# A two-layer SSM and attention kernel: one gate job of the first layer moved into the opening

## The chip, the cores and the metric

The kernel runs on one core of one Trainium2 chip. The metric is the device time of one execution in microseconds (us): the median of several runs. Everything is float32.

## The reference

A token block of 512 x 2048 goes through two layers of a first block (an S5 state-space mixer beside a differential attention, joined by an output projection) and through a second block (gated delta rule beside sliding-window attention). Only the start of layer one matters here, cut to:

```python
c_act = silu(c)
mod = c_act @ w_ada[l] + b_ada[l]                 # w_ada: 2048 x 6144
shift, scale, gate = split(mod, 3)
h = rms_norm(x, norm_g[l]) * (1 + scale) + shift
proj = h @ w_in[l]                                # 2048 x 6144
u, z_s, q, k, v, z_a = split(proj, ...)           # 1024 columns each
y_s = s5_mixer(u, ...) * silu(z_s)                # the state chain
q, k = rope(q), rope(k)
y_a = diff_attention(q, k, v, ...) * silu(z_a)
x = x + gate * (concat(y_s, y_a) @ w_out[l])
```

In this document layer one is `l = 0` of the code.

## The kernel before, in words

**One plan, five walks.** The program first writes one list of steps (`plan`, by `do(...)`), and then each engine (TensorE, VectorE, ScalarE, GpSimd, and SyncE as the main DMA queue) walks that list and issues its own part of each step, with semaphore waits. So each engine runs its instructions strictly in the order of the plan. `Room` hands out tiles of a ring first in, first out: `take`, `give`, and `clear` for what the next tenant has to wait for. There are 8 PSUM banks (`banks` and `aux` are the same ring), 4 weight slots of 1 MB (`wslots`), 14 temporary tiles of 128 x 512 (`temps`) and 4 slots of 1 MB for the opening's modulation weights (`aslots`).

**The opening** (`start`, line 673 on). x is loaded and turned, and the norm's square sum is made with ones-matmuls. Then shift and scale of layer one are computed in four quarters j, each 512 columns of shift and of scale. A quarter has four parts (k0 = 0, 4, 8, 12). In each part VectorE multiplies and adds 1 MB of scale weights (`first_sum`, four instructions), and TensorE puts 1 MB of shift weights through a matmul (`first_row`, four matmuls, two records each). The 32 transfers of 1 MB (`first_fetch`, SyncE queue) run four ahead: the next one waits until the VectorE or TensorE step that reads its slot is done. When quarter j is complete, `close(j)` (planned behind the first `first_sum` of the next quarter) folds it with 16 one-column matmuls (`first_turn`), VectorE adds biases (`first_out`), and ScalarE applies scale and shift to four tiles of h (`norm_shift`). The tiles of h of quarter j are the contraction rows for quarter j of the products. So the first product, `u_job(0, 0)` (512 columns of u, four token tiles, four PSUM banks held throughout), goes along a quarter behind: `step_group(group, j - 1)`, one step (one tile, four contraction blocks, 8 matmul records) behind each of the parts k0 = 4, 8, 12, and `run_all` for the rest at the end of the quarter.

**The state parameters** (`state_space_params(0)`, called `prep` here). A generator with nine yields. In the kernel before, the quarters advance it twice each, eight times: (1) fetch of the small tables; (2) fetch of C, their turn on TensorE, and VectorE's exponential; (3) to (6) more small VectorE work, with the fetches of B at (4) and (6); (7) the turn of C (`c_turn`: 16 transposes, 8 VectorE copies) and the last parameters; (8) GpSimd's `powers` and `angles`, VectorE's `c_power`; (9), after the opening, VectorE's `angle_turn` and ScalarE's `sine`.

**After the opening** (`block_one`). The last quarter of the group runs. Then the plan has `rope` (ScalarE first issues the load of the positions and of the lambda vectors, `late_fetch`; VectorE computes the angle; ScalarE the sine) and `lambda`. Then steps of `beside_states` ("beside" steps: 16 of the second half of u, then 32 of the attention gate z_a, then 32 of the state gate z_s, 80 in all) run on TensorE: five of them ahead of `turn_u(0, 0)`, the other 75 between the steps of `state_space(0)` by `interleave`, 73/79 of a step per yield. In an iteration k of the state chain TensorE's parts are `e_turn` (transposes of Est), `drive`, `lags`, `add_up` and `y_turn`; between `y_turn` and the next-but-one `drive` there is a chain over VectorE (scan, rotations, `c_power`, angle), ScalarE (sine, Em) and GpSimd. Ahead of the first `e_turn` ScalarE has, in this order, the sine of iteration 0, four copies of `turn_u` and `e_place` (tile Est).

**A gate job** (`gate_products`) is 2 tiles x 4 = 8 steps and two weight blocks of 1 MB. At a tile's end ScalarE runs `save_z`: it waits for the bank, applies Silu, and issues the store to DRAM. `modulation` (the ada weights of later stages, on the GpSimd queue and VectorE) is carried along by the steps of `dense`, 1.35 of its own steps per step here; the steps of a group don't carry it.

All matmuls are issued at line 108 and all transposes at line 111; VectorE's, ScalarE's and GpSimd's helpers are lines 116 to 150, DMAs line 153. The tiles tell the steps apart: `yaT`, `SS`, `side` hold the opening's ada weights, `wring` the product weights, `region_b` is h, `region_a` x and later u.

Of the kernel before, what the change touches and what calls it, by code (L numbers as in the profile page):

```python
# [15 lines left out]
P = 128  # L16
# [260 lines left out]
def build(nc, d, out, at, ncols):  # L277
    ctx = ExitStack()
    with ctx:
# [393 lines left out]
        def start():  # L673
# [34 lines left out]

            def close(j):
                do("first_turn", j)  # L710
                temps.give("acc", 0, j)
                temps.give("arow", j)
                do("first_out", j)
                for k in range(4 * j, 4 * j + 4):
                    do("norm_shift", 0, k)
            group = open_group([u_job(0, 0)])
            aux.take("mod", 0)
            for j in range(4):
                temps.take("acc", 0, j)
                load_group(group, j)  # L720
                aux.take("row", j)
                temps.take("arow", j)
                steps_ = step_group(group, j - 1) if j else iter(())
                for k0 in range(0, KT, 4):
                    do("first_sum", j, k0)
                    aslots.give("first", SCALE, j, k0)
                    fetch()
                    if j and k0 == 0:
                        close(j - 1)
                    do("first_row", j, k0)  # L730
                    aslots.give("first", SHIFT, j, k0)
                    fetch()
                    if k0:
                        next(steps_, None)
                    if k0 % 8:
                        next(prep, None)
                run_all(steps_)
                if j == 0:
                    temps.take("r", 0)
                    do("norm_root", 0)  # L740
                    aux.give("norm", 0)
                for k in range(4 * j, 4 * j + 4):
                    do("norm_scale", 0, k)
                do("first_keep", j)
                aux.give("row", j)
            do("x_store", 0)
            close(3)
            aux.give("mod", 0)
            temps.give("wide_c")
            temps.give("r", 0)  # L750
            do("fence", "h", 0)
            run_all(step_group(group, 3))
            do("fence", "start")
            return prep
# [97 lines left out]
        def beside_states(l):  # L852
            open_split(l)
            yield from dense(u_job(l, 512))
            for h0 in range(0, HT, 2):
                for n, _ in enumerate(gate_products(l, h0, "za", 5 * HALF)):
                    if h0 == 0 and n == 3:
                        turn_u(l, 512)
                        do("pe_fence", "u", l)
                    yield  # L860
            for h0 in range(0, HT, 2):
                quarter(h_split[l], h0, 2)
                do("quarter_rest", h_split[l], h0, 2)
                yield from gate_products(l, h0, "zs", HALF)

        def gate_products(l, h0, name, n0):
            job = layer_dense(l, d["w_in"][l], n0 + h0 * P, "save_z", h0, name)
            for j in range(2):
# [246 lines left out]
        def block_one(l):  # L1115
# [28 lines left out]
            do("pe_fence", "first_u", l)  # L1144
            interleave(state_space(l), beside, [73, 77][l] / 79)
            do("fence", "ssm", l)
# [391 lines left out]
        def tensor():  # L1538
# [107 lines left out]
            def first_turn(j):  # L1646
                bank, acc, row = aux.at("mod", 0), temps.at("acc", 0, j), temps.at("arow", j)
                if j == 0:
                    room(aux.clear("mod", 0))
                    pe.wait_ge(*d_ones.of())  # L1650
# [339 lines left out]
        def vector():  # L1990
# [182 lines left out]
            def first_out(j):  # L2173
                bank, a, z = aux.at("mod", 0), 4 * j, 4 * j + 4
                dve.wait_ge(*ada_turned.of("first", j))
# [5 lines left out]
                    *ada_ready.up("first", j))  # L2181
                aux.leave(("mod", 0), dve.mine())

# [1414 lines left out]
```

## Time and profile before

| | us |
|---|---|
| median of 3 runs (4060.53 to 4062.89) | 4061.3 |
| the profiled execution's own time | 4058.25 |
| its span | 4056.3 |
| TensorE busy in the span | 3950.0 (97%) |
| VectorE / ScalarE / GpSimd busy | 2478.8 / 900.2 / 508.0 |
| mean granted TensorE clock | 0.991 |

The span is from the first to the last instruction; 1.95 us of the execution's time lie around it. In timelines a row is a start, a duration, the engine, the line, the operation with out<-in, the count, and in brackets the idle time just before with what ended it. PE is TensorE, DVE VectorE, ACT ScalarE, POOL GpSimd, SP SyncE; ACTq and SPq are DMA issues of those queues. One step of a product is 8 matmul records.

### The profile page before, as it was taken

The page shows a single profiled execution, that of the slowest core. Times are in us where ns is not written, and L with a number is a line of the kernel's source. Part 1 is how long each engine was busy: PE and PEld are TensorE (multiplying, and loading weights), DVE is VectorE, ACT ScalarE, POOL GpSimd, SP SyncE. Part 2 cuts the span into 40 slices and gives each one's busy share as a digit, 9 for nine tenths or more (in the row PEclk, how much of TensorE's full clock was granted, in tenths as well). Part 3 has the DMA queues.
Part 4 walks back from the last instruction along what each step waited for, and adds up shares of the span by engine and source line. Part 5 has one row for each costly group of instructions (what it writes and reads, how often), then busy time and mean ns, then how long its engine had stood idle before and what let it go on. Part 6 is the DMA issues. An engine that isn't in the chain of part 4 may idle for free.

```text
span 4056.3 us, 46566 instructions
## 1 busy us (share of the span) xinstructions
PE 3950.0 (97%) x18296; PEld 3047.9 (75%) x18296; DVE 2478.8 (61%) x4446; ACT 900.2 (22%) x1643; POOL 508.0 (13%) x808
## 2 busy tenths in 40 slices
PE   6999999999999999999999999999999999999999
PEld 3665598855877556987468578888888888888888
DVE  6667658776763675688665456363645356756643
ACT  2222212342021222123411222131312123220000
POOL 0233211111122341112110000000000101100000
PEclk8999999999999999999999999999999999999999
DMA  9643344444652332443444341212222334434423
GB/s 335 208 136 111 117 133 141 125 143 148 187 176 78 125 121 98 155 136 121 144 161 139 113 125 48 72 63 68 73 68 78 112 104 133 129 109 132 140 96 107
DMA packets 382951, 508.01 MB, mean 125 GB/s; under 512 B 44827, under 2 KB 296078, under 8 KB 382222
## 3 DMA queue, kind: packets, MB, share of 16 engines
q1 hardware_dynamic: 300544, 344.36, 26.3%
q0 software_dynamic: 38480, 125.86, 10.1%
q10 hardware_dynamic: 43710, 34.83, 2.7%
q8 instruction: 145, 2.38, 0.2%
q14 instruction: 72, 0.59, 0.0%
HBM read 466.71 MB, written 38.27 MB: 124 GB/s over the span
## 4 chain that ended last, share of the span: by engine, by line
PE 83%; DVE 11%; ACT 2%; issue 2%; DMA 1%; ACTq 0%; DVEq 0%; SPq 0%; POOL 0%
PE bank L108 80%; PE bank L111 2%; DVE tring L129 2%; DVE wring L123 2%; DVE tring L123 2%; ACT tring L116 1%; DMA side<-in_w_ada 1%; DVE bank L123 1%; DVE dring L123 1%; DVE tring L126 0%; DVE sring L144 0%; DVE region_b L123 0%; DVE dring L126 0%; DVE region_a L123 0%; DVE s_delta L123 0%
## 5 line engine op out<-in xcount | busy, mean ns | idle before, releaser
L108 PE MATMUL bank<-region_b,wring 128*128 128x256 f32 (+1 forms) x4416 | 1194.0, 424 | 7.2 <-ACT region_b L116 3.9
L108 PEld LDWEIGHTS bank<-region_b,wring 128*128 128x128 f32 x4416 | 825.5, 190 | 298.6 <-issue 204.1
L108 PE MATMUL bank<-region_a,wring 128*128 128x256 f32 (+1 forms) x3360 | 926.8, 429 | 3.7 <-DVE wring L123 3.7
L108 PEld LDWEIGHTS bank<-region_a,wring 128*128 128x128 f32 x3360 | 628.0, 190 | 236.3 <-issue 165.2
L123 DVE TENSOR_TENSOR tring<-bank,tring 128x256 f32<-128x256 f32 (+1 forms) x325 | 141.6, 436 | 435.8 <-PE bank L108 432.4
L116 ACT ACTIVATE tring<-bank 32x512 f32<-32x512 f32 (+2 forms) x341 | 177.8, 523 | 984.3 <-PE bank L108 565.2
L123 DVE TENSOR_TENSOR wring<-wring 128x1024 f32<-128x1024 f32 (+1 forms) x309 | 354.9, 1149 | 24.5 <-PE bank L108 13.2
L153 POOL DMA_DIRECT2D side<-in_w_ada x384 | 209.0, 545 | 1280.8 <-DVE tring L129 826.3
L129 DVE SCALAR_TENSOR_TENSOR tring<-side,cact,tring 128x512 f32<-128x512 f32 x360 | 304.6, 846 | 50.7 <-DMA side<-in_w_ada 12.7
L123 DVE TENSOR_TENSOR bank<-bank,tring 128x256 f32<-128x256 f32 (+1 forms) x309 | 160.0, 518 | 119.2 <-PE bank L108 115.6
L108 PE MATMUL bank<-wring,region_b 128*128 128x128 f32 (+2 forms) x896 | 212.8, 396 | 7.3 <-ACT region_b L116 7.3
L108 PEld LDWEIGHTS bank<-wring,region_b 128*128 128x128 f32 x896 | 161.9, 227 | 58.8 <-issue 26.8
L108 PE MATMUL bank<-wring,region_a 128*128 128x128 f32 (+1 forms) x768 | 173.9, 386 | 3.2 <-ACT region_a L116 3.2
L108 PE MATMUL bank<-yaT,wring 128*128 128x256 f32 x768 | 175.1, 383 | 1.8 <-DMA wring<-in_w_out 1.8
L116 ACT ACT_TABLE_LOAD x109 | 139.8, 1283 | 135.7 <-DVE sring L126 54.8
L108 PEld LDWEIGHTS bank<-wring,region_a 128*128 128x128 f32 x768 | 137.1, 231 | 36.8 <-issue 6.7
L108 PEld LDWEIGHTS bank<-yaT,wring 128*128 128x128 f32 x768 | 145.4, 192 | 25.1 <-issue 5.7
L123 DVE TENSOR_TENSOR tring<-tring 128x512 f32<-128x512 f32 (+2 forms) x142 | 99.5, 701 | 85.7 <-ACT tring L116 80.4
L116 ACT ACTIVATE tring<-tring 128x512 f32<-128x512 f32 x145 | 88.0, 627 | 259.9 <-DVE tring L126 196.5
L116 ACT ACTIVATE tring<-bank,sring 128x128 f32<-128x128 f32 (+3 forms) x128 | 67.5, 527 | 309.9 <-DVE sring L126 309.8
L108 PE MATMUL bank<-outT,wring 128*128 128x256 f32 x512 | 113.7, 379 | 0.0
L108 PEld LDWEIGHTS bank<-outT,wring 128*128 128x128 f32 x512 | 97.0, 190 | 13.5 <-DVE wring L123 0.5
(317 smaller groups left out, 4735.7 us busy)
## 6 DMA issues: line engine op xcount, KB each, us to landing
wring<-in_w_in SPq DMA_DIRECT2D x178, 1024.0 KB, 5.3
side<-in_w_ada POOLq DMA_DIRECT2D x384, 256.0 KB, 3.1
wring<-in_w_out SPq DMA_DIRECT2D x48, 1024.0 KB, 7.6
yaT<-in_w_ada SPq DMA_DIRECT2D x16, 1024.0 KB, 9.3
wring<-in_w_glu SPq DMA_DIRECT2D x16, 1024.0 KB, 7.5
tring<-x_saved SPq DMA_DIRECT2D x48, 256.0 KB, 3.1
gring<-in_w_ada POOLq DMA_DIRECT2D x43, 256.0 KB, 3.1
SS<-in_w_ada SPq DMA_DIRECT2D x8, 1024.0 KB, 9.3
```

The source lines that it names most:

```text
L108: return self.e.matmul(*a, **k) if self.e else self
L111: return self.e.transpose(*a) if self.e else self
L116: return self.e.activation(o, x, f, **k) if self.e else self
L123: return self.e.tensor_tensor(*a) if self.e else self
L129: return self.e.scalar_tensor_tensor(out=o, in0=a, scalar=s, in1=b, op0=op0, op1=op1) if self.e else self
L153: return self.e.dma_start(dst, src, allow_slow_non_contiguous=True) if self.e else self
```

## The change

The first attention gate job of layer one (`h0 = 0`, 256 columns, "za") becomes a second member of the opening's group. Its two tiles hold two banks through the opening, each quarter has six steps instead of four, and its two weight blocks are loaded with quarters 0 and 2. Since 4 + 2 + the norm's bank + the row's bank are all eight, the `mod` bank is taken and given per quarter, and `prep` isn't advanced in quarter 0: the quarters advance it six times instead of eight, and (7) to (9) come behind `rope` and `lambda`, each with one beside step. The gate is left out of `beside_states`, which has 72 steps then: 7 ahead of `turn_u(0, 0)` and 65 in the interleaving, at 65/79 of a step per yield.

```diff
@@ start
             def close(j):
+                aux.take("mod", j)
                 do("first_turn", j)
                 temps.give("acc", 0, j)
                 temps.give("arow", j)
                 do("first_out", j)
+                aux.give("mod", j)
                 for k in range(4 * j, 4 * j + 4):
                     do("norm_shift", 0, k)
-            group = open_group([u_job(0, 0)])
-            aux.take("mod", 0)
+            group = open_group([u_job(0, 0), gate_job(0, 0, "za", 5 * HALF)])
...
-                    if k0 % 8:
+                    if j and k0 % 8:
                         next(prep, None)
...
             close(3)
-            aux.give("mod", 0)
             temps.give("wide_c")
             temps.give("r", 0)
             do("fence", "h", 0)
+            for n in range(2):
+                temps.take("za", 0, n)
             run_all(step_group(group, 3))
+            for n in range(2):
+                temps.give("za", 0, n)
             do("fence", "start")
@@ beside_states
-            for h0 in range(0, HT, 2):
+            done = 0 if l else 2
+            for h0 in range(done, HT, 2):
                 for n, _ in enumerate(gate_products(l, h0, "za", 5 * HALF)):
-                    if h0 == 0 and n == 3:
+                    if h0 == done and n == 3:
                         turn_u(l, 512)
...
+        def gate_job(l, h0, name, n0):
+            return layer_dense(l, d["w_in"][l], n0 + h0 * P, "save_z", h0, name)
@@ block_one
-            interleave(state_space(l), beside, [73, 77][l] / 79)
+            interleave(state_space(l), beside, [65, 77][l] / 79)
@@ first_turn (TensorE), first_out (VectorE): the same bank per quarter
-                bank, acc, row = aux.at("mod", 0), temps.at("acc", 0, j), temps.at("arow", j)
+                bank, acc, row = aux.at("mod", j), temps.at("acc", 0, j), temps.at("arow", j)
+                room(aux.clear("mod", j))
```

## Rows read from the trace of the kernel before

**Rows 1.** The page: busy time of each engine over the span.
```profile
PE 3950.0 (97%) x18296; PEld 3047.9 (75%) x18296; DVE 2478.8 (61%) x4446; ACT 900.2 (22%) x1643; POOL 508.0 (13%) x808
```
**Rows 2.** Windows: length, busy us per engine (count), clock, DMA share, GB/s.
```profile
100.00:120.00 20.00, 19.63 (x70) 10.60 (x67) 15.60 (x42) 3.53 (x5) 0.00 (x0) 0.84 1.11 357
...
140.00:160.00 20.00, 14.20 (x35) 9.07 (x36) 7.27 (x13) 2.93 (x4) 2.48 (x3) 0.74 0.51 174
...
320.00:360.00 40.00, 40.00 (x148) 22.03 (x147) 28.49 (x40) 11.52 (x17) 14.61 (x23) 1.00 0.33 109
```
**Rows 3.** Timeline of TensorE, the opening and the start of the states.
```profile
85.96 1.84 PE L108 MATMUL bank<-ones,tring 128*128 128x1 f32 x16
...
113.97 1.84 PE L108 MATMUL bank<-ones,tring 128*128 128x1 f32 x16
...
132.17 7.26 PE L108 MATMUL bank<-wring,region_b 128*128 128x512 f32 x16
139.26 1.84 PE L108 MATMUL bank<-ones,tring 128*128 128x1 f32 x16
146.91 33.55 PE L108 MATMUL bank<-wring,region_b 128*128 128x512 f32 x72 [5.80 <-ACT region_b L116]
180.29 1.91 PE L111 MATMUL bank<-const,region_a 128*128 128x128 f32 x16
184.27 1.09 PE L111 MATMUL bank<-const,Est 128*128 128x128 f32 x8 [2.06 <-ACT Est L116]
```
**Rows 4.** Timeline of TensorE in the state stage.
```profile
357.37 17.33 PE L108 MATMUL bank<-region_b,wring 128*128 128x512 f32 x40
374.53 1.04 PE L111 MATMUL bank<-const,Est 128*128 128x128 f32 x8
...
384.06 1.95 PE L108 MATMUL bank<-region_a,Em 128*128 128x128 f32 x16
```
**Rows 5.** Waits of the TensorE and SyncE queues, 0 to 150 and 160 us.
```profile
PE bank L108 <- DMA yaT<-in_w_ada: 12.9, 3, 5.8
PE bank L108 <- DMA side<-in_w_ada: 10.0, 5, 3.5
...
SPq L153 <- DVE mod L123: 10.1, 1, 10.1
```
**Rows 6.** Issue to landing: tile `wring` to 165 us, and the positions.
```profile
DMA to landing us min/median/max: 5.2/12.7/14.2
...
tring<-in_positions ACTq DMA_DIRECT2D x1, 256.0 KB, 3.7
```
**Rows 7.** Timeline of VectorE: turn of C, rope's start, first angle.
```profile
124.00 3.60 DVE L132 COPY CT<-bank 64x256 f32<-64x256 f32 x8 [4.50 <-PE bank L111]
...
130.78 3.18 DVE L129 SCALAR_TENSOR_TENSOR tring<-yaT,cact,tring 128x512 f32<-128x512 f32 x4
...
163.94 0.42 DVE L132 CAST tring<-tring 128x512 f32<-128x512 int32 x1
...
175.14 0.89 DVE L126 TENSOR_SCALAR tring<-tring 128x512 f32<-128x512 f32 x2
```
**Rows 8.** Timeline of ScalarE and its DMA issues.
```profile
145.95 0.81 ACT L116 ACTIVATE region_b<-region_b,mod 128x512 f32<-128x512 f32 x1 [12.99 <-DVE mod L129]
145.96 0.35 ACTq L153 DMA_DIRECT2D tring<-in_positions  x1
...
178.70 1.15 ACT L116 ACTIVATE tring<-tring 128x512 f32<-128x512 f32 x2 [3.25 <-DVE tring L126]
...
355.66 0.33 ACTq L153 DMA_DIRECT2D za_saved<-tring  x1
...
377.70 1.07 ACT L116 ACTIVATE Em<-bank 128x512 f32<-128x512 f32 x2
```
**Rows 9.** Timeline of GpSimd: powers (12 instructions) and angles, and powers again.
```profile
130.77 0.29 POOL L123 TENSOR_TENSOR W<-cf,Bn 128x64 f32<-128x64 f32 x1 [126.25 <-DVE cf L123]
...
139.49 0.72 POOL L123 TENSOR_TENSOR W<-W,tg 128x192 f32<-128x192 f32 x1
...
141.53 1.17 POOL L123 TENSOR_TENSOR tring<-th,const_one 128x512 f32<-128x512 f32 x1
...
182.70 0.30 POOL L123 TENSOR_TENSOR W<-cf,Bn 128x64 f32<-128x64 f32 x1
...
188.47 0.59 POOL L123 TENSOR_TENSOR W<-W,tg 128x192 f32<-128x192 f32 x1
```

More of the change, by code:

```diff
@@ L864, in beside_states @@
                 yield from gate_products(l, h0, "zs", HALF)
+        def gate_job(l, h0, name, n0):
+            return layer_dense(l, d["w_in"][l], n0 + h0 * P, "save_z", h0, name)
         def gate_products(l, h0, name, n0):
-            job = layer_dense(l, d["w_in"][l], n0 + h0 * P, "save_z", h0, name)
+            job = gate_job(l, h0, name, n0)
             for j in range(2):
@@ L1646, in first_turn @@
             def first_turn(j):
-                bank, acc, row = aux.at("mod", 0), temps.at("acc", 0, j), temps.at("arow", j)
+                bank, acc, row = aux.at("mod", j), temps.at("acc", 0, j), temps.at("arow", j)
+                room(aux.clear("mod", j))
                 if j == 0:
-                    room(aux.clear("mod", 0))
                     pe.wait_ge(*d_ones.of())
@@ L2173, in first_out @@
             def first_out(j):
-                bank, a, z = aux.at("mod", 0), 4 * j, 4 * j + 4
+                bank, a, z = aux.at("mod", j), 4 * j, 4 * j + 4
                 dve.wait_ge(*ada_turned.of("first", j))
@@ L2181, in first_out @@
                     *ada_ready.up("first", j))
-                aux.leave(("mod", 0), dve.mine())
+                aux.leave(("mod", j), dve.mine())
             def ada_total(m, n0):
```

## The prediction

> **What bounds the kernel now.** I read the page first: TensorE is busy 97% of the span [rows 1], so what TensorE doesn't have to do, or does where it would idle, is what a change can earn. Then the windows by stage. In the state stage TensorE has no idle time at all, at full clock: 40.00 of 40 us [rows 2]. A step taken out of that stage is worth its whole length. The opening is different. In 100 to 120 us TensorE is busy but the clock is 0.84 and DMA is saturated at 357 GB/s; in 140 to 160 us TensorE idles 5.8 us [rows 2]. The waits say for what: up to 150 us TensorE lost 12.9 + 10.0 = 22.9 us to the ada weights [rows 5]. Last, the timelines of the seam between the two, which is where the stages hand over: h is complete and the last quarter starts at 146.91 (call this moment S), and the state chain's first `e_turn` starts at 184.27, S + 37.4, after a wait of 2.06 us for ScalarE's Est [rows 3].
>
> **The change part by part.** I sum on the profiled execution (4058.25 us, 3.05 us below the median of 4061.3) and carry the difference over to the median. A step in the state stage takes (374.53 - 357.37) / 5 = 3.43 us [rows 4]; in the quarters two take 139.26 - 132.17 = 7.09 us, 3.55 each [rows 3]. The gate job's eight steps are 27.4 us of TensorE. Two of them come after S, six go into quarters 1 to 3.
>
> *Term 1, the opening: when does S come?* Folds stand at 85.96, 113.97 and 139.26 [rows 3]. A quarter gets 7.1 us more TensorE work, all of it behind its last `first_row`: four steps in a row there (14 us) instead of two. Quarter 1: against the 7.1 us stands that VectorE's exponential moves from quarter 0 to the end of quarter 1. SyncE stood 10.1 us behind VectorE with the next ada transfer there [rows 5], and most of that goes; I take 4 us back, so the fold comes at 89. Quarter 2: TensorE's floor is the fold 1.84, four rows of about 1.07 and six steps, 27.4 us. The transfer for the third part is issued only when the first row is through, and needs 5.2 us at best [rows 6] where a row and a step cover 4.6, and the fourth queues behind it: some 1.5 us. 29 us, fold at 118. Quarter 3: 29 again, fold at 147; the turn of C is gone from it, and the floor does not count it. Then fold and hand-over, 1.84 + 1.5, put S' near 150.5 to 151, since VectorE's `c_power` no longer stands ahead of the last scaling (5.8 us of idle before S now, [rows 3]). **S' - S = 4.** Bounds: 2 (all fits as above with the idle gone), and 14 if the added steps hide nothing (3 x 7.1, less 3 for the turn of C, less 4.3 of the final idle). I take 4, since 22.9 us of waits and an 0.84 clock stand in the stretch to be filled. The 2 MB of gate weights I cost at nothing: block 0 goes into the time before 36 us in which TensorE still sums squares, block 2 into the steps at the end of quarter 1, where the queue otherwise waits for TensorE. Without that cover they cost 1.05 MB / 357 GB/s = 2.9 us each [rows 2]. The B tables go two yields later than before and are needed long after.
>
> *Term 2, the seam.* Here I count every queue that is passed. TensorE has, from S', 6 group steps, 7 beside steps, 16 transposes of C (as 16 in 1.91 us, [rows 3]) and `turn_u` 1.9: it stands at `e_turn` at S' + 48.4; with the 2.1 us that ScalarE needs behind it, 50.5. But the chain feeding `e_turn` has grown. ScalarE now has two `save_z` in front of `rope`. The second one waits for the gate's last step, S' + 20.7, then Silu 0.6 and a store 0.33 [rows 8], and only then does ScalarE issue the positions, at S' + 21.8; before, they were issued at 145.96, just ahead of S [rows 8], and VectorE had them when it came to them. They land 3.7 us later [rows 6]: 25.5. From rope's cast to the first angle VectorE took 175.14 - 163.94 = 11.2 us (rope, lambda, one ada sum) [rows 7]: 36.7. Now comes the turn of C and the last parameters, 130.78 - 124.00 = 6.8 us [rows 7]: 43.5. GpSimd's powers and angles wait for those parameters: 130.77 to 142.70, 11.9 us [rows 9]: 55.4. VectorE's angle, 178.7 - 175.14 = 3.5: 59. ScalarE's sine, its four copies and Est, up to `e_turn`, 184.27 - 178.70 = 5.6 us [rows 8, 3]: 64.5. GpSimd may be quicker: the same 12 powers took 188.47 + 0.59 - 182.70 = 6.4 us where VectorE was mostly idle, 9.4 at 130.77 where it was busy [rows 9]; beside `c_power` I take a value between, 8. So **`e_turn` starts at S' + 63**, against S + 37.4: 25.6 us more between the two marks. Bounds: 50.5, where all is covered, and 65. The Trainium skill (SBUF — State Buffer, Who interferes with whom) says that GpSimd and VectorE fight for a port that one holds alone while VectorE reads two SBUF inputs; the two durations agree, and by it alone the powers beside `c_power` would be nearer 9.4, `e_turn` at 64.5 and the time 1.5 us higher.
>
> *Term 3, what is left behind that mark.* 75 steps before, 72 - 7 = 65 after: **-10 x 3.43 = -34.3 us**.
>
> *Term 4, cover in the state stage.* 65/79 in place of 73/79 leaves one step less in most iterations. Counting the yields, between `y_turn` and the `drive` it feeds stand 7, 7, 6, 6, 7, 7, 6 steps before and 6, 6, 6, 6, 5, 6, 6 after. The one with 5 had 7: Em ended at 378.77 and the drive began at 384.06 [rows 8, 4], 5.3 us of slack against 6.9 us taken. That gives 1.6 us of wait, less an ada sum or two that VectorE no longer has in it. **+1**, from 0 to 4 (a microsecond each in the tighter ones).
>
> *Term 5, the clock.* After 5.80 us idle TensorE took 33.55 us for nine steps that take 30.9 [rows 3, 4]: 2.6 us lost to a lower granted clock. A wait of 14 us ahead of `e_turn` costs about as much again: **+2**, 0 to 2.6. The loss at S itself goes, since the gap there shrinks; it is in term 2, which counts from S' at full clock.
>
> *The rest at nothing:* the bank per quarter (its former tenants have been read long before); the later slots for the second half of u (the last block is issued at S' + 20.7 and needed three steps on, 10.3 us, where 5.2 do [rows 6], as now); ten modulation steps that are carried later and have spare steps behind them in the layer.
>
> Sum: 4 + 25.6 - 34.3 + 1 + 2 = **-1.7 us**. From 4058.25 that is 4056.5 for a profiled execution, and from the median 4061.3 about **4059**. In words: 20.6 us leave the saturated stage, the opening takes them for some 4 us, and most of the rest is spent waiting at the seam. About 0.2% (8 us) is what a measurement of this kernel can tell from no change.
>
> **The rivals.** *A, the seam is covered.* If the chain ran fast enough, `e_turn` would come at S' + 50.5: 4 + 13.1 - 34.3 + 1 = -16.2, 4045. If only the positions came in time (say the store and Silu don't hold them), VectorE could start rope at S' + 14.6 (now S + 17.0, 2.5 of it slow clock) and the same sum gives S' + 53.6: 4 + 16.2 - 34.3 + 1 = -13, 4048. For it speaks that every part of the chain is short and TensorE has 13 steps of work meanwhile; against it that the sum of parts, each a row, is 12 us too long, and that now the sine ends only when TensorE arrives (178.70 against 180.29, [rows 8, 3]), so there is no slack to eat. *B, the opening is serial, slower.* Its mechanism is SyncE's one queue: in quarter 3 the load of u's last block waits for a slot that is free only after four steps of the bunch, ada transfers queue behind it, and each shift transfer waits for a TensorE that is in its bunch. Then the added steps hide nothing, 14 us, and the 2 MB cost 5.8 more: 19.8 + 25.6 - 34.3 + 1 + 2 = +14, 4075. It decides when S' - S is over 14. Against it: VectorE's sums don't depend on the bunch, and three transfers of 1 MB are in flight during it. *C, the granted clock.* At 0.84 in 100 to 120 us [rows 2] some 3 us per quarter are slow clock; with six steps per quarter TensorE idles less and could run at 2.4 GHz throughout, which would make S' - S as little as -2 and the time 4053. The Trainium skill (TensorE: Matmul & The Clock Gate, Part 1) says that activity is what releases the throttle, which points that way; the trace agrees in that the clock is 1.00 in the state stage. But the waits for rows 8 and 12 of each quarter stay, so I keep 4.
>
> **How the numbers follow.** The seam wait as worked out: 0.64 (4052 to 4066). Rival A with its partial form: 0.24. Rival B: 0.08. Rival C: 0.04. Faster by over 0.2% (under 4053) is A and the low end of the forecast: 0.28. Slower (over 4069) is B: 0.07. Within: 0.65. The range leaves out B, the lower tail of A and little else: 4046 to 4066.
>
> **What would show it.** In the changed kernel's timeline of TensorE: folds near 89, 118 and 147; matmuls of the last quarter from about 151, six steps in a row there with no wait over 2 us; then a wait of 10 to 15 us at the first transposes of Est, released by ScalarE. On ScalarE the issue of the positions must stand behind the second za store, 21 to 23 us after S'. On GpSimd the first powers start 43 us after S'. In the state stage one wait of 1 to 2 us for Em. I am wrong if TensorE's wait at Est stays under 5 us (then A), or if S' is later than 160 (then B).

## The result, and the profile after

| | before | after |
|---|---|---|
| median of 20 runs each, same chip | 4064.12 us (4058.53 to 4072.6) | 4070.03 us (4066.66 to 4078.51) |
| ratio, 95% interval | | 1.0015 (1.0009 to 1.0021) |
| the profiled execution's own time | 4058.25 | 4078.51 |
| its span | 4056.3 | 4076.7 |

The change costs 5.9 us, 0.15%: too little for the 0.2% that I had called a difference, but plainly on the slow side, and 4 us above the top of my range. 2.8 of those 4 us come from the kernel before, whose median rose from 4061.3 with 3 runs to 4064.1 with 20; against its own base the change was forecast at -1.7 us with a top of +4.7, and measured +5.9. One run of seam_again, a kernel further down, was slow (4589.9 us) and is in no number here. One thing must be said before any row is compared. The two profiled executions lie on opposite sides of their medians: that of before 5.9 us under, that of after 8.5 us above. They differ by 20 us where the medians differ by 5.9. So I compare stages, and take sizes from the ratios of the runs where there are any.

The page: TensorE is busy 11 us longer than before [rows 1], with the same number of records. It does the same work, slower.

```profile
PE 3961.0 (97%) x18296; PEld 3055.6 (75%) x18296; DVE 2481.3 (61%) x4446; ACT 901.8 (22%) x1644; POOL 514.1 (13%) x808
```

Windows of the three quarters, from fold to fold (columns as in [rows 2]):

```profile
53.00:93.00 40.00, 33.00 (x100) 17.44 (x100) 22.21 (x54) 3.53 (x5) 0.00 (x0) 0.83 1.07 365
93.00:125.00 32.00, 28.28 (x95) 15.17 (x95) 20.44 (x55) 5.37 (x9) 0.00 (x0) 0.95 1.09 353
125.00:158.00 33.00, 30.33 (x97) 15.57 (x97) 18.01 (x53) 3.54 (x5) 0.00 (x0) 0.90 0.86 283
```

The same stretch in TensorE's timeline, against [rows 3]. In quarter 3 the third row of the sum waits 2.67 us for its transfer. The row itself and the step behind it are slow ones, 1.94 us in place of 1.07 and 5.94 in place of the 3.82 of the step ahead of the wait; from 143.12 on the matmuls are at full speed again.

```profile
92.79 1.84 PE L108 MATMUL bank<-ones,tring 128*128 128x1 f32 x16
...
125.27 1.84 PE L108 MATMUL bank<-ones,tring 128*128 128x1 f32 x16
...
128.89 3.82 PE L108 MATMUL bank<-wring,region_b 128*128 128x512 f32 x8
135.39 1.94 PE L108 MATMUL bank<-yaT,tring 128*32 128x512 f32 x8 [2.67 <-DMA yaT<-in_w_ada]
137.25 5.94 PE L108 MATMUL bank<-wring,region_b 128*128 128x512 f32 x8
143.12 1.06 PE L108 MATMUL bank<-side,tring 128*32 128x512 f32 x8
144.12 7.26 PE L108 MATMUL bank<-wring,region_b 128*128 128x512 f32 x16
...
158.07 1.84 PE L108 MATMUL bank<-ones,tring 128*128 128x1 f32 x16
161.38 15.79 PE L108 MATMUL bank<-wring,region_b 128*128 128x512 f32 x32 [1.46 <-ACT region_b L116]
...
209.77 1.91 PE L111 MATMUL bank<-const,region_a 128*128 128x128 f32 x16
229.56 1.94 PE L111 MATMUL bank<-const,Est 128*128 128x128 f32 x8 [17.88 <-ACT Est L116]
231.29 4.91 PE L108 MATMUL bank<-wring,region_b 128*128 128x512 f32 x8
```

So S' is 161.38 (before 146.91), and the first `e_turn` starts at 229.56 after a wait of 17.88 us, where before it waited 2.06 us at 184.27. Behind it TensorE has no idle time at all for 290 us: its only wait between 200 and 520 us is this one.

```profile
PE bank L111 <- ACT Est L116: 17.9, 1, 17.9
```

The chain in front of that wait is the one that I had written down. ScalarE, the second za store and behind it the positions, the sine, Est (against [rows 8]):

```profile
184.13 0.60 ACT L116 ACTIVATE tring<-bank 128x512 f32<-128x512 f32 x1 [2.90 <-PE bank L108]
184.76 0.34 ACTq L153 DMA_DIRECT2D za_saved<-tring  x1
185.13 0.46 ACTq L153 DMA_DIRECT2D tring<-in_positions  x1
...
224.41 1.15 ACT L116 ACTIVATE tring<-tring 128x512 f32<-128x512 f32 x2 [20.08 <-DVE tring L126]
...
228.14 1.28 ACT L116 ACTIVATE Est<-W 64x512 f32<-64x512 f32 x2
```

VectorE: it stands 14.95 us for the positions, turns C only afterwards, and then waits for GpSimd (against [rows 7]):

```profile
192.84 0.43 DVE L132 CAST tring<-tring 128x512 f32<-128x512 int32 x1 [14.95 <-DMA tring<-in_positions]
...
203.91 3.59 DVE L132 COPY CT<-bank 64x256 f32<-64x256 f32 x8
...
220.85 0.89 DVE L126 TENSOR_SCALAR tring<-tring 128x512 f32<-128x512 f32 x2 [5.88 <-POOL tring L123]
```

GpSimd's twelve powers and the second angle (against [rows 9]); the powers end at 218.52, 7.5 us after their start:

```profile
211.03 0.59 POOL L123 TENSOR_TENSOR W<-cf,Bn 128x64 f32<-128x64 f32 x1 [3.00 <-DVE cf L123]
...
217.93 0.59 POOL L123 TENSOR_TENSOR W<-W,tg 128x192 f32<-128x192 f32 x1
...
219.78 1.04 POOL L123 TENSOR_TENSOR tring<-th,const_one 128x512 f32<-128x512 f32 x1
```

From before to after `e_turn` moves by 45.3 us, and 10 steps fewer stand behind it. Of the 45.3, 2.4 us have nothing to do with the change: quarter 0's fold already stands at 53.02 in place of 50.64, because in that execution the turn of x ahead of it took 6.2 us in place of 3.7, at a granted clock of 0.58 in place of 1.00. The norm's sum behind that turn starts between 21.3 and 21.8 in nine of the fourteen profiles of this study, at 23.0 to 24.6 in the other five, without a pattern by kernel.

### The profile page after: what moved, and what is told of

It is laid out like the page before. It is cut to its first block, busy times and chain, and to the rows that moved or that the text cites. A ratio compares the mean times of both kernels' runs of the same rounds, so it can differ in the third digit from the quotient of the medians.

```text
span 4076.7 us, 46580 instructions
## 1 busy us (share of the span) xinstructions
PE 3961.0 (97%) x18296; PEld 3055.6 (75%) x18296; DVE 2481.3 (61%) x4446; ACT 901.8 (22%) x1644; POOL 514.1 (13%) x808
## 4 chain that ended last, share of the span: by engine, by line
PE 82%; DVE 11%; ACT 2%; DMA 2%; issue 2%; POOL 0%; ACTq 0%; DVEq 0%; SPq 0%; POOLq 0%
PE bank L108 80%; PE bank L111 2%; DVE tring L129 2%; DVE wring L123 2%; DVE tring L123 2%; DMA side<-in_w_ada 1%; ACT tring L116 1%; DVE bank L123 1%; DVE dring L123 1%; DVE tring L126 1%; DVE sring L144 0%; DVE dring L126 0%; DVE region_a L123 0%; DVE s_delta L123 0%; DVE outT L123 0%
## 5 line engine op out<-in xcount | busy, mean ns | idle before, releaser
L108 PEld LDWEIGHTS bank<-outT,wring 128*128 128x128 f32 x512 | 97.0, 190 | 14.5 <-DVE wring L123 1.4
```

What stands on the lines that cost most here:

```text
L108: return self.e.matmul(*a, **k) if self.e else self
```

## The experiments

All ratios are to the kernel before on the same chip. The change has 20 runs, seam, best and seam_again have 5, the others 11. The edits are against the changed kernel unless it is said otherwise. The columns of the table are those on which the readings rest: the length of quarters 1, 2 and 3 (from fold to fold in TensorE's timeline), the start of the last quarter's steps, and the wait at the first transposes of Est with the time at which it ended.

| kernel | ratio (95%) | median | quarters 1, 2, 3 | S or S' | wait, ended at |
|---|---|---|---|---|---|
| before | 1 | 4064 to 4068 | 35.3, 28.0, 25.3 | 146.9 | 2.1, 184.3 |
| the change | 1.0015 (1.0009 to 1.0021) | 4070.0 | 39.8, 32.5, 32.8 | 161.4 | 17.9, 229.6 |
| after_again | 1.0016 (1.0007 to 1.0025) | 4072.5 | 40.5, 33.2, 31.0 | 159.3 | 17.7, 227.3 |
| positions_first | 0.9985 (0.9976 to 0.9994) | 4059.4 | 40.2, 32.3, 30.5 | 156.1 | 5.5, 211.9 |
| params_late | 1.0024 (1.0015 to 1.0032) | 4076.4 | 34.2, 30.7, 29.9 | 147.0 | 9.7, 198.5 |
| b_late | 1.0005 (0.9996 to 1.0014) | 4067.0 | 40.7, 29.5, 28.5 | 151.9 | 17.0, 219.1 |
| c_late | 1.0007 (0.9999 to 1.0016) | 4065.6 | 37.7, 31.6, 31.0 | 153.5 | 17.0, 220.7 |
| spread | 1.0007 (0.9998 to 1.0016) | 4068.4 | 35.1, 37.2, 27.5 | 153.1 | 18.1, 222.6 |
| rope_early | 0.9994 (0.9985 to 1.0003) | 4060.7 | 40.3, 32.3, 30.9 | 158.8 | 5.2, 212.6 |
| all_in | 0.9973 (0.9964 to 0.9982) | 4053.4 | 37.9, 28.7, 28.5 | 148.4 | 6.8, 205.5 |
| seam | 0.9954 (0.9940 to 0.9968) | 4044.3 | 37.8, 28.7, 28.8 | 148.5 | 2.1, 200.6 |
| seam_again | 0.9957 (0.9943 to 0.9971) | 4045.2 | 37.8, 28.6, 28.4 | 147.9 | 2.1, 200.3 |
| best | 0.9951 (0.9938 to 0.9963) | 4043.8 | 35.0, 33.3, 27.0 | 149.9 | 2.2, 202.8 |
| seam_no_gate | 0.9990 (0.9981 to 0.9999) | 4060.0 | 31.6, 28.5, 27.9 | 142.5 | 3.4, 191.9 |

**after_again.** The changed kernel once more, for a second profile.

> The changed kernel once more, unchanged, for its spread. In its profile the last quarter's matmuls began at 161.4 us and TensorE waited 17.9 us at the first turn of Est (229.6), but that execution was 8 us above the median, and 3.2 us of it lay ahead of the quarters. Theory 1 (the quarters and the seam are what costs, both fixed by the order of the work): last quarter about 158 to 161, wait 17 to 18 us again, 1.0015 times the kernel before. Theory 2 (the seam's wait is a matter of that one execution): the wait comes out under 14 us.

It repeats: 1.0016, a wait of 17.73 us, S' = 159.3. The shape isn't an accident of one execution.

**positions_first.** The positions are issued ahead of the last quarter's steps, so that they don't stand behind the two za stores.

```diff
             do("fence", "h", 0)
+            for name in ("pos", "lam"):
+                temps.take(name)
+            do("late_fetch")
...
-            for name in ("pos", "ang", "turns", "lam"):
+            for name in ("ang", "turns"):
                 temps.take(name)
```

(and the call of `late_fetch()` taken out of ScalarE's `rope`).

> The changed kernel with one thing undone: ScalarE issues the load of the positions and the lambda vectors behind the last norm_shift, as in the kernel before, and not behind the two save_z. Theory 1 (the positions held behind save_z are the longest limb of the seam): rope's cast starts at S' + 16.5 instead of S' + 31.5, then the wait for the start fence on ScalarE holds it to S' + 24, so C's copies start 12 to 13 us earlier, the wait at Est falls from 17.9 to about 5 us and the kernel is 12 to 14 us faster than the changed one (4056 to 4058), faster than the kernel before by about 0.2%. Theory 2 (the limb through C, the parameters and GpSimd's powers decides by itself, since they come behind lambda and ada fetches): the wait stays above 12 us and the time within 4 us of the changed kernel.

The wait shrinks to 5.54 us and the ratio falls by 0.0031, 12.6 us of 4065. The first theory holds: the queue of ScalarE, not the arithmetic, makes most of the wait.

```profile
156.06 15.79 PE L108 MATMUL bank<-wring,region_b 128*128 128x512 f32 x32 [1.46 <-ACT region_b L116]
...
211.90 1.94 PE L111 MATMUL bank<-const,Est 128*128 128x128 f32 x8 [5.54 <-ACT Est L116]
```

**params_late.** The kernel before with one condition changed: the parameters aren't advanced in quarter 0, and nothing else moves. The gate job stays beside the state chain.

```diff
-                    if k0 % 8:
+                    if j and k0 % 8:
                         next(prep, None)
```

> The kernel before with nothing but the later parameters: they are not advanced in quarter 0, so steps 7 to 9 come behind rope and lambda; no gate job in the group, positions in time, 80 beside steps of which 7 stand ahead of turn_u. Theory 1 (the moved parameters alone put a wait at the seam): S comes 3 to 5 us earlier (142 to 144), the first turn of Est waits about 10 us at S + 53, and the kernel is 3 to 8 us slower than before. Theory 2 (the later parameters are covered by the seven steps, and only the positions cost): wait at Est under 5 us and the time within 2 us of before or up to 5 us faster.

This has the highest ratio of the study: 1.0024, about 10 us slower than before, where I had expected 3 to 8. Its quarters 2 and 3 take 30.7 and 29.9 us with four steps in each, where before takes 28.0 and 25.3, and at the seam it waits 9.73 us.

```profile
147.00 17.53 PE L108 MATMUL bank<-wring,region_b 128*128 128x512 f32 x40 [1.45 <-ACT region_b L116]
...
198.48 1.94 PE L111 MATMUL bank<-const,Est 128*128 128x128 f32 x8 [9.73 <-ACT Est L116]
```

So the part of the change that looks like bookkeeping, six turns for `prep` in place of eight, costs by itself as much as the whole change or more (the intervals of 1.0024 and 1.0015 overlap). The gate job itself must be earning: between this kernel and positions_first, which has the gate job and the positions in time, stand 0.0039, some 16 us.

**b_late and c_late.** In each, one set of table loads is issued behind the opening's products instead of beside the ada stream.

```diff
             do("fence", "h", 0)
+            do("ssm_fetch", 0, 2)
+            do("ssm_fetch", 0, 3)
```

(b_late, and parts 2 and 3 left out of `prep`; c_late is the same with part 1.)

> The changed kernel with the two loads of the B tables (256 KB in 64-byte pieces, 20 and 28 us to land) issued behind the last norm_shift instead of in quarters 2 and 3. Quarters 2 and 3 took 32.5 and 32.8 us from fold to fold where I had worked out 29. Theory 1 (the small pieces slow the 1 MB transfers that the third row of a quarter waits for, and the waits bring the slow clock): both quarters 29 to 30.5 us, time 4 to 6 us below the changed kernel. Theory 2 (the quarters are long because each shift transfer is issued only when TensorE is out of its bunch): quarters within 1 us of 32.5, time within 2 us. In both the wait at Est may shift, since its chain starts at S' anyway: no change of it.

> The changed kernel with the eight loads of C (1 MB in all, in 256-byte rows) issued behind the last norm_shift and not in quarter 1. Quarter 1 (fold to fold) was 35.3 us in the kernel before, 39.8 to 40.5 us in four kernels with the gate job in the group, and 34.2 us in the one with only the parameters moved. Theory 1 (C's loads share quarter 1 with the ada weights; they left quarter 0, where DMA had room): quarter 1 is 37 us or less, time 2 to 4 us below the changed kernel. Theory 2 (quarter 1 is long because of its four steps in a row alone): quarter 1 within 1 us of 40 and the time as the changed kernel's. The wait at Est stays 17 to 18 us in both.

b_late: quarters 2 and 3, 29.5 and 28.5 us in place of 32.5 and 32.8, quarter 1 as it was. The windows show full clock in both, with the same six steps (against 0.95 and 0.90 above):

```profile
90.00:120.00 30.00, 27.70 (x98) 15.55 (x97) 21.04 (x56) 5.37 (x9) 0.00 (x0) 1.00 0.96 347
120.00:150.00 30.00, 28.69 (x111) 16.77 (x109) 18.00 (x53) 3.53 (x5) 0.00 (x0) 1.00 0.97 347
```

c_late: quarter 1, 37.7 us in place of 39.8 to 40.7, the others nearly as they were. The C loads take 13.2 and 17.8 us from issue to landing in the changed kernel, 2.8 and 2.9 in c_late, and took 2.5 and 2.8 before, where they ran in quarter 0. The changed kernel:

```profile
tring<-in_ssm_c_re ACTq DMA_DIRECT2D x4, 128.0 KB, 13.2
tring<-in_ssm_c_im ACTq DMA_DIRECT2D x4, 128.0 KB, 17.8
```

Each is worth about 0.001, 4 us, by its ratio (the intervals overlap that of the change). So the loads' place is one term of the opening, and it is additive. The three quarters sum to 102.9 to 105.1 us, 104.0 in the mean, in the four kernels with the six steps and all the loads in place (the change, after_again, positions_first, rope_early). b_late is 5.3 below that mean, c_late 3.7, and all_in, which has both, 8.9: 95.1 us.

**spread.** Two product steps behind each of parts 4, 8 and 12 of a quarter, none left for a bunch at its end.

```diff
-                    if k0:
-                        next(steps_, None)
+                    for _ in range(2 if k0 else 0):
+                        next(steps_, None)
```

> The changed kernel with the six steps of a quarter placed 2, 2, 2 behind the parts k0 = 4, 8, 12 instead of 1, 1, 4. Theory 1 (the bunch of four starves the shift transfers, and the waits for them bring the slow clock): the waits for the third row (2.3 to 3.7 us in quarters 2 and 3) vanish, quarters 2 and 3 take 28 to 30 us where they took 31 to 33, time 4 to 7 us below the changed kernel. Theory 2 (transfers are short of bandwidth beside the B tables, whatever the order of the steps): the waits move to the fourth row, quarters within 1 us of the changed kernel's.

Quarters 1 to 3 sum to 99.8 us, 5 less than the change; the ratio says 1.0007. Quarter 1 gains 5 us, and in quarter 3 the wait for the third row goes down to 0.50 us and the quarter to 27.5, as theory 1 had it. But in quarter 2, where it forecast 28 to 30 us, TensorE now asks for the tiles of h before ScalarE has written them:

```profile
97.14 9.04 PE L108 MATMUL bank<-wring,region_b 128*128 128x512 f32 x16 [7.36 <-ACT region_b L116]
```

The bunch costs something in quarter 1 and covers the hand-over of h in quarter 2. With the loads out of the way and `prep` at other places (best, below) nothing is left of the gain.

**rope_early.** Rope and lambda with their loads go ahead of the last quarter altogether.

```diff
             do("fence", "h", 0)
+            for name in ("pos", "ang", "turns", "lam"):
+                temps.take(name)
+            do("late_fetch")
+            do("fence", "rope")
+            do("rope")
+            do("lambda")
+            for name in ("pos", "ang", "turns", "lam"):
+                temps.give(name)
```

(and out of the place behind it).

> The changed kernel with the positions' load, rope and lambda planned right behind the last norm_shift, ahead of the group's last quarter, so that neither the two save_z nor rope stand ahead of the turn of C. With the positions alone in time the wait at Est was still 5.5 us (of which 2.06 belong to ScalarE's own copies). Theory (the seam is one chain and its limbs add): C's copies on VectorE start when TensorE has turned it, S' + 25 instead of S' + 30, the wait at Est is 2 to 2.5 us and the time 2 to 4 us below positions_first, 4055 to 4057. Rival (GpSimd's own part, ada fetches and three memsets ahead of the powers, is the next limb): the wait stays 4 us or more.

A miss. The wait is 5.19 us, hardly better than in positions_first, and the ratio is no lower (0.9994 and 0.9985, the intervals overlap). VectorE is done with rope early and then stands for a modulation transfer that GpSimd issues only at 181.16. The turn of C comes behind that, at S' + 28.2, where positions_first has S' + 30.2 and I had expected S' + 25.

```profile
186.58 0.48 DVE L126 TENSOR_SCALAR tring<-side,cact 128x512 f32<-128x512 f32 x1 [11.92 <-DMA side<-in_w_ada]
186.99 3.59 DVE L132 COPY CT<-bank 64x256 f32<-64x256 f32 x8
```

**all_in** is rope_early with the C and B loads behind the fence.

> rope_early with the loads of C and B behind the last norm_shift as well, to see whether the parts add: opening 6 to 10 us shorter (S' 150 or less), wait at Est 2 to 5 us (C and B must land first: C within 5 us, B within 28 us of S'). If they add, 4046 to 4051, 0.3 to 0.45% below the kernel before. If B's landing becomes a limb (powers start later than S' + 32), the gain over rope_early is under 3 us.

0.9973, 4053.4 us, 2 us above the range that I had given, and the wait is still 6.80 us: the positions stand behind ten table loads on ScalarE's queue, and VectorE waits 14.85 us for them (cast at 162.30).

**seam** takes away both waits that the last two showed: the positions are issued ahead of the C and B loads, and the other modulations are planned behind the last of `prep`.

```diff
             do("late_fetch")
+            do("ssm_fetch", 0, 1)
+            do("ssm_fetch", 0, 2)
+            do("ssm_fetch", 0, 3)
             do("fence", "rope")
...
-                behind.extend([modulation(m) for m in range(1, 5)])
                 next(beside)
                 for _ in prep:
                     next(beside)
+                behind.extend([modulation(m) for m in range(1, 5)])
```

> all_in with two changes at the seam: the later modulations (their fetches on GpSimd, their sums on VectorE) are carried only once the parameters are through, and ScalarE issues the positions ahead of the loads of C and B. In rope_early and all_in VectorE stood 11.9 us in front of C's copies, at an ada sum whose transfer had waited for the start fence. Theory (that sum is the limb that was left): C's copies start at S' + 25 where they started at S' + 28 and S' + 31, the wait at Est is 2 to 3 us, and the kernel is 3 to 6 us below all_in: 4048 to 4050. Rival (the landing of B, 20 to 28 us in small pieces, is next): the powers wait for B and the wait at Est stays at 5 us or more.

0.9954, and 0.9957 the second time: 17 to 19 us faster than before, some 24 us faster than the change. The turn of C is at 174.71, VectorE now waits for TensorE's transposes and not the other way round, and `e_turn` waits 2.14 us, as much as before the change:

```profile
148.49 15.44 PE L108 MATMUL bank<-wring,region_b 128*128 128x512 f32 x32 [1.46 <-ACT region_b L116]
...
200.58 1.06 PE L111 MATMUL bank<-const,Est 128*128 128x128 f32 x8 [2.14 <-DVE tring L129]
```

**best** is seam with spread, and `prep` advanced six times at other parts of the quarters.

> seam with the quarters rearranged: six steps as 2, 2, 2 behind the parts, and the first parameter step (only the fetch of the small tables, which needs no bank) back in quarter 0, so that VectorE's exponential stands behind the second part of quarter 1 and not between its end and the scaling of h. In spread quarters 1 to 3 took 35.1, 37.2 and 27.5 us; the 37.2 held a wait of 7.4 us for h. Theory (that wait was the exponential ahead of the last scaling): quarters of about 35, 29 and 27.5 us, S' about 144 to 146, time 2 to 5 us below seam, about 0.4% below the kernel before. Rival (two steps behind every part delay the rows and so the transfers): quarters 1 and 2 add up to more than 66 us and nothing is gained on seam.

0.9951: the same as seam within the intervals. Its quarters sum to 95.3 us, those of seam to 95.2. The gain that I expected didn't come: quarter 2 takes 33.3 us and not 29, and quarters 1 and 2 add up to 68.3, on the side of the rival.

**seam_no_gate and seam_again.** seam with the gate job taken back out of the opening (`open_group([u_job(0, 0)])`, one `mod` bank, 73/79, the gate beside the state chain), and seam itself on the same chip.

> The version with the positions, C and B loads and angles pulled ahead (0.9954 of before), with the gate job taken back out of the opening's group: the opening is before's with its parameters moved, and the gate tiles stand beside the state chain again. Theory: with the seam covered the gate job in the opening is worth what it was worth between the two earlier kernels that differ by it with the positions in time (0.9985 against 1.0024, -0.0039, 16 us). Then this kernel is 12 to 20 us slower than the version with it, ratio to before 0.9984 to 1.0003, and its quarters 1 to 3 are 4 to 7 us shorter each in all but the first. Rival: the gain of that version is the earlier loads' alone, and the gate job in the group is neutral: within 5 us of it, ratio 0.9942 to 0.9966.

> The same kernel as the version with the loads, rope and angles pulled ahead, once more on the same chip as the one without the gate job, so that the two are compared directly: 0.9945 to 0.9963 of before if its first measurement holds.

0.9990 against 0.9957: the gate job in the opening is worth 0.0033, 13.4 us, once nothing else is in its way (with both intervals, 7 to 20 us). One part of the expectation was wrong. I expected the six steps to lengthen quarters 2 and 3 and leave the first alone; it is the other way round. Quarter 1 is 6.2 us longer with the gate (37.8 and 31.6), quarters 2 and 3 only 0.1 and 0.7 us (28.65 and 28.5, 28.6 and 27.9, with the mean of the two profiles of seam). Of seam_no_gate's quarter 2, TensorE's timeline shows where the two steps go. It has a wait of 4.08 us for h, 8.5 us behind the fold at 82.72. In seam the fold comes behind the two added steps, VectorE is through with the exponential by then, and the first step starts 3.6 us behind the fold without a wait:

```profile
91.22 5.84 PE L108 MATMUL bank<-wring,region_b 128*128 128x512 f32 x8 [4.08 <-ACT region_b L116]
```

The window of its quarter 2 stands at clock 0.88, and that of seam at 1.00, and both last 28.6 us:

```profile
82.70:111.30 28.60, 22.72 (x83) 12.38 (x81) 26.34 (x72) 5.37 (x9) 0.00 (x0) 0.88 0.84 303
```

```profile
87.80:116.40 28.60, 27.17 (x97) 15.32 (x96) 20.51 (x55) 5.37 (x9) 0.00 (x0) 1.00 0.90 324
```

## Why the prediction was wrong, point by point

The parts and the place of the wait were right; the sum was short by 7.6 us (-1.7 forecast, +5.9 measured), and the range ended below the result. Of the signs that I had named, the wait at Est was released by ScalarE as forecast, but was 17.9 us (10 to 15), the positions were issued 23.75 us after S' (21 to 23), the first powers started 49.65 us after it (43), and S' was later than 160 in one of the two profiles (161.4 and 159.3). By its steps:

**Term 1, S' - S, is the step that failed.** Forecast 4, bounds 2 to 14. From quarter 0's fold to the start of the last quarter's steps (which leaves out the 2.4 us ahead of it) before takes 146.91 - 50.64 = 96.3 us and the change 161.38 - 53.02 = 108.4: **+12.1**, in after_again +11.6. What I had wrong is the price of the loads that move with the parameters, which I put at nothing: "the B tables go two yields later than before and are needed long after", and no word on the C tables. With my folds at 89, 118 and 147 quarters 1 to 3 would take 96.4 us. With the C and B loads out of them the changed quarters do take 95.1 to 95.2 (all_in, seam), and with the loads in 102.9 to 105.1. So the loads cost 8 to 10 us, and the term was short by 8.1. (That the rest fits so well is in part luck: the gate's steps cost less in quarters 2 and 3 than I had allowed, and an open 2.6 us in quarter 3, below, stands in their place.) The hand-over behind the last fold was forecast at 3.34 us and took 3.31 (before 7.65).

- By the edits singly, and from the start of quarter 0's fold to S': the move of the parameters adds 6.2 us to the quarters (params_late less before) and takes 4.4 off the hand-over, the gate adds 8.1 (positions_first less params_late). That is +10.0; the change itself had 2.1 us more in one execution of the same quarters.
- The two added steps per quarter cost 6.0, 1.6 and 0.6 us (positions_first less params_late), or 6.2, 0.1 and 0.7 without the table loads. In quarters 2 and 3 the gate is all but free. In quarter 1 nothing hides it: the last row of the sum starts as early with the gate as without (22.6 us behind the fold in seam, 23.2 in seam_no_gate), and from there to the next fold it is 15.2 and 8.3 us. The steps stand serially there. That the row isn't later also bears out that the 2 MB of gate weights cost nothing in that quarter.
- The four microseconds that I "took back" in quarter 1 for VectorE's exponential don't show: params_late, which makes that move alone, has 34.2 in place of 35.3. SyncE's 10.1 us wait for VectorE [rows 5] did go, but the eight loads of C came into the same quarter with the exponential. Without them (seam_no_gate) the quarter takes 31.6, 3.8 us less than before; before has one of the two B loads in it as well, so this isn't the exponential alone.
- The move of the parameters costs quarters 2 and 3 another 2.7 and 4.6 us with no gate step in them (params_late). b_late shows 2 to 4 us a quarter for a B load. But the B loads were issued in quarters 1 and 2 before (61.80 and 88.31) and are in quarters 2 and 3 now, so that can explain most of quarter 3's share and nothing of quarter 2's. There TensorE waits 1.31 us for h, as it does for longer in seam_no_gate and not at all before; whether that is the whole of it isn't shown. Even with the loads gone, quarter 3 stays 2.6 us above the 25.3 of before (27.9 in seam_no_gate). What makes that up is open.

**Term 2, the seam, right in every link and 5 us short.** `e_turn` at S' + 63 by forecast, S' + 68.2 in the change, S' + 68.0 in after_again. The positions were issued at S' + 23.75 (21.8 forecast) and took 7.7 us to land (3.7 [rows 6]); that is 6 us by the cast. From cast to the turn of C it took 11.1 us, by forecast 11.2. The powers took 7.5 (8). Of these the first six took 3.25 us, beside VectorE's `c_power`, and the seventh, the first of 192 columns, 1.00 beside an ada sum; the next set of powers, with VectorE idle, did the same six in 2.22 and the seventh in 0.53:

```profile
214.36 1.00 POOL L123 TENSOR_TENSOR W<-back,W 128x192 f32<-128x192 f32 x1
...
228.54 0.31 POOL L123 TENSOR_TENSOR W<-cf,Bn 128x64 f32<-128x64 f32 x1
...
230.84 0.53 POOL L123 TENSOR_TENSOR W<-back,W 128x192 f32<-128x192 f32 x1
```

But `c_power` ends long before the twelve do, so the price here was 1.5 us (7.5 less the 6.0 of that next set) and not the 3 between 6.4 and 9.4. The Trainium skill (SBUF — State Buffer, Who interferes with whom) says that a VectorE instruction with two SBUF inputs contends with a GpSimd instruction that reads SBUF; the trace agrees.

Both ends of my bounds (50.5 and 65) were for the arithmetic; none was for the landing of the positions, which I took from one row. Over the fourteen profiles they landed in 3.4 to 3.7 us five times and in 6.8 to 7.9 us nine times.

**Term 3**, 10 steps fewer behind the mark: as forecast. **Term 4** was 0 and not +1: no wait for Em. **Term 5** was 2.4 us by the rows (8 transposes in 1.94 in place of 1.04, a step in 4.91 in place of 3.43), forecast 2.

With these sizes the sum is 12.1 + (68.2 - 37.4) - 34.3 + 0 + 2.4 = **+11.0**, and the trace agrees: at the first pair products of the state chain (512.96 before, 525.33 after) the change is 12.4 us behind, 2.4 of them from ahead of the quarters, so 10. The medians say 5.9. The 4 to 5 us between are not settled: loads and clock vary by microseconds from one execution to the next, and the one profile of before is 6 us under its own median. Both kernels have issued the same 1693 records of matmuls and transposes by that mark; what is behind it takes between 3542 and 3553 us in the fourteen profiles, in no order by kernel.

**Rival A** (faster) is what the experiments built. Its partial form, the positions in time, was forecast 11.3 us below the main sum and measured 12.6 below. Its full form, `e_turn` covered, was forecast 14.5 below; seam stands 24 below the change: its quarters are 10 us shorter as well (95.2 and 105.1 in all), and its `e_turn` comes at S' + 52.1 in place of 68.2. **Rival B** (serial, slower) had the right sign, and its mechanism was right in one part of three. S' - S came near its threshold of 14 (12.1, or 14.5 with the 2.4 us from ahead of the quarters). SyncE's queue for u's last block and the 2 MB of gate weights aren't the cause: with both still there, seam's S' is 148.5. The bunch of steps is one, in quarter 1 as above, and in quarter 3, where the wait for the third row (2.67 and 2.27 us in the two profiles of the change) is 0.50 with the steps spread and 0.73 with the B loads gone: either alone removes it. **Rival C** (the clock) had a point that the change itself couldn't show: its quarters 2 and 3 ran at 0.95 and 0.90, and at 1.00 with the B loads gone (b_late), but also with them in place and C's gone (c_late).

## What to carry to other kernels

When a step is moved, list the transfers that move with it and price them in the stretch that they arrive in, not by when their data is needed. A load that is issued from an engine's own queue is as late as the compute instructions in front of it, and this is cheap to cure: issue it as a step of its own, ahead of them. And test the parts alone before judging the whole: here a change that lost 6 us was one that earns 13 to 16, with a companion that costs 10 and a queue order that costs 12.

## What the runs showed of the hardware

- The C tables are 1 MB, and their loads beside the ada stream take 13 to 18 us to land in seven profiles, against 2.5 to 3.6 us in the seven in which they run elsewhere. They cost the stream 2 to 3 us, about what 1 MB takes at the 365 GB/s of that window (2.9 us). The B tables are half as large and cost as much or more: 2 to 4 us a quarter for 256 KB, which at that rate are 0.7 us. The Trainium skill (DMA: Bandwidth & Descriptors, Specifications) gives 512 bytes as the least piece for full rate; the kernel loads C in pieces of 256 bytes and B in pieces of 64, and the dearer B agrees with it, while C, below that size too, cost no more than its bytes. No run here loads the same bytes in larger pieces, so that cause is argued and not shown.
- The granted clock followed the gaps, but no length of a wait divides the cases. The six steps of quarter 2 or 3, in the order 1, 1, 4, stood at 0.90 to 0.95 (part of the stretch at 1.2 GHz, part at 2.4) where the longest wait was 2.27 to 3.65 us, and at 1.00, all at 2.4, where it was up to 2.56. That 2.56 is c_late's quarter 2, a longer wait at full clock than the 2.27 of after_again's quarter 3, which stood at 0.94:

```profile
97.59 1.07 PE L108 MATMUL bank<-yaT,tring 128*32 128x512 f32 x8 [2.56 <-DMA yaT<-in_w_ada]
```

```profile
87.58:119.21 31.63, 27.23 (x98) 15.36 (x96) 20.54 (x55) 5.37 (x9) 0.00 (x0) 1.00 1.03 335
```

- The two added steps of quarters 2 and 3, 7 us of matmuls each, lengthen them by 0.1 and 0.7 us, since they take the place of idle time and of slow clock. In quarter 2 TensorE idles 5.9 us in seam_no_gate and 1.4 in seam, and seam_no_gate's first step takes 5.84 us in place of 3.82.
- The same 256 KB of positions landed in 3.4 us or in 7.9. seam and best issue them in the same place, at 147.54 and 148.92, and had 3.5 and 7.9. The 3.4 us behind the issue in each:

```profile
147.54:150.94 3.40, 2.45 (x3) 1.22 (x4) 0.00 (x0) 2.92 (x4) 0.00 (x0) 0.57 0.28 82
```

```profile
148.92:152.32 3.40, 2.46 (x3) 1.22 (x4) 0.00 (x0) 2.91 (x4) 0.00 (x0) 0.65 1.05 402
```

Four of the five short landings had 82 to 84 GB/s of traffic in that stretch, and eight of the nine long ones 264 to 402. Two don't fit: before had 296 and landed in 3.7, and all_in had 96 and took 7.3, behind ten table loads of its own queue. So the traffic goes with the landing time, but isn't shown to be all of it.
